# Two transformer blocks in one launch: who makes the last tile sum of a seven-product set, and where the activation sums are made

## The reference, cut to what matters

```python
hf = rms_norm(x, g_ffn[layer])
x = x + (jax.nn.silu(hf @ w_gate[layer]) * (hf @ w_up[layer])) @ w_down[layer]
...
h2 = rms_norm_2(x, g_ffn[i])
x = x + (jax.nn.silu(h2 @ w_gate[i]) * (h2 @ w_up[i])) @ w_down[i]
```

## Time and profile before

| what | value |
|---|---|
| median of 3 runs | 2364.06 us (2363.55 to 2365.42) |
| the profiled execution, its own time | 2367.7 us |
| its span in the trace | 2365.9 us |
| granted TensorE clock, mean | 0.998 of full |
| busy: PE, weight loads, DVE | 99%, 83%, 82% |
| busy: ACT, POOL | 52%, 17% |

### The profile page before, as it was taken

The page is one execution under the profiler, slowest core; times in us unless marked ns, Lnnn a source line. Parts: engine busy times, 40 slices in busy tenths (PEclk is TensorE's granted clock), DMA queues, the critical chain, the costliest instruction groups (busy, mean ns, idle before and its releaser), DMA issues.

```text
span 2365.9 us, 30942 instructions
## 1 busy us (share of the span) xinstructions
PE 2352.9 (99%) x10692; PEld 1957.8 (83%) x10692; DVE 1948.9 (82%) x2542; ACT 1223.9 (52%) x1639; POOL 403.6 (17%) x290
## 2 busy tenths in 40 slices
PE   9999999999999999999999999999999999999999
PEld 8988888878888788888888888888888888888887
DVE  7788887889888877878897976988988897787885
ACT  6554555645454544545654445455545454464553
POOL 1000000130534335200000000013053433520000
PEclk9999999999999999999999999999999999999999
DMA  8755455656766666665655564566575766665655
GB/s 304 238 176 186 153 170 167 222 196 189 248 203 233 204 228 226 213 213 187 195 196 196 178 196 160 194 239 204 186 251 198 242 213 236 216 214 200 212 190 168
DMA packets 130338, 487.44 MB, mean 206 GB/s; under 512 B 14480, under 2 KB 15120, under 8 KB 129568
## 3 DMA queue, kind: packets, MB, share of 16 engines
q1 hardware_dynamic: 116736, 421.32, 53.6%
q0 software_dynamic: 13184, 64.02, 7.6%
q10 hardware_dynamic: 288, 0.33, 0.0%
HBM read 483.51 MB, written 2.10 MB: 205 GB/s over the span
## 4 chain that ended last, share of the span: by engine, by line
PE 65%; DVE 3%; issue 0%; ACT 0%; ACTq 0%; DVEq 0%
PE acc L627 43%; PE po L627 7%; PE pt L627 6%; PE acc L774 3%; PE pt L774 2%; PE po L774 2%; DVE w_lo L1654 1%; DVE tmp_c L1789 1%; PE acc L664 0%; PE po L965 0%; PE acc L904 0%; PE acc L889 0%; PE po L973 0%; DVE tmp_b L1709 0%; ACT w_hi L1145 0%
## 5 line engine op out<-in xcount | busy, mean ns | idle before, releaser
L1654 DVE TENSOR_TENSOR w_lo<-raw,w_hi 128x1024 fp32r<-128x1024 f32 x796 | 1033.3, 1313 | 299.0 <-ACT w_hi L1145 292.2
L1145 ACT ACTIVATE w_hi<-raw 128x1024 fp32r<-128x1024 f32 x795 | 833.4, 1058 | 797.9 <-PE acc L627 499.2
L627 PE MATMUL acc<-w_hi,norm_hi 128*128 128x512 f32 (+1 forms) x1460 | 568.5, 390 | 0.1
L627 PE MATMUL acc<-w_hi,norm_lo 128*128 128x512 f32 (+1 forms) x1460 | 565.3, 387 | 0.0
L627 PE MATMUL acc<-w_lo,norm_hi 128*128 128x512 f32 (+1 forms) x1460 | 387.5, 387 | 0.0
L627 PE MATMUL acc<-w_hi,mix_hi 128*128 128x512 f32 x832 | 325.1, 391 | 0.8 <-DVE mix_lo L2153 0.8
L627 PE MATMUL acc<-w_hi,mix_lo 128*128 128x512 f32 x832 | 324.0, 389 | 0.0
L627 PEld LDWEIGHTS acc<-w_hi,norm_hi 128*128 128x128 f32 x1460 | 274.2, 188 | 55.8 <-issue 0.8
L627 PEld LDWEIGHTS acc<-w_hi,norm_lo 128*128 128x128 f32 x1460 | 274.2, 188 | 55.1
L627 PEld LDWEIGHTS acc<-w_lo,norm_hi 128*128 128x128 f32 x1460 | 272.9, 188 | 56.0 <-DVE w_lo L1654 0.2
L627 PE MATMUL acc<-w_lo,mix_hi 128*128 128x512 f32 x832 | 222.6, 389 | 0.2 <-DVE w_lo L1654 0.2
(11 more groups left out here) (354 smaller groups left out, 2934.8 us busy)
## 6 DMA issues: line engine op xcount, KB each, us to landing
raw<-stream SPq DMA_DIRECT2D x795, 512.0 KB, 3.7
heads<-seven_in POOLq DMA_DIRECT2D x48, 768.0 KB, 6.9
heads<-seven_in POOLq DMA_DIRECT2D x12, 512.0 KB, 7.4
tab<-seven_in POOLq DMA_DIRECT2D x12, 512.0 KB, 7.4
heads<-x_in POOLq DMA_DIRECT2D x4, 512.0 KB, 9.0
x<-x_tok POOLq DMA_DIRECT2D x4, 512.0 KB, 7.1
x<-mem_tok POOLq DMA_DIRECT2D x2, 1024.0 KB, 6.6
x<-x_tok POOLq DMA_DIRECT2D x1, 2048.0 KB, 10.1
```

Of the source, the lines that this page charges most:

```text
L627: last = pe.matmul(out_[:, c * NB:c * NB + width], a[:, k * T + c * P:k * T + (c + 1) * P], w[:, s, kk * width:(kk + 1) * width], start=cl ...
L1145: act.activation(w_hi[:, (units.fixed - 1) % RING, :], src, ACT.Copy).then_inc(w_hi_ready, 1)
L1654: dve.tensor_tensor(w_lo[:, s, :], src, w_hi[:, s, :].bitcast(F32), ALU.subtract)\
```

## The change

There are three edits.

1. POOL makes three of the four sums of a step. The fourth, the last tile, is made by DVE for both steps at once, as one subtraction of 128x1024 (`last_sums`), placed right ahead of part 0 of `seven_lo`. It waits for the load of the last tile and for POOL's sums of both steps. ACT's copy of the last tile (line 1245) waits for it (`last_summed`).
2. The norm sums move from pair (0, "up", 1) to the end of the pair before it. In (0, "up", 1) the parts of `seven_lo` stand at splits 6, 8 and 10 instead of 6, 8 and 11.
3. The hidden sums of group 1 move from pair (1, "up", 2) to (1, "up", 1). In both pairs that have hidden sums `sums_raw` stays at split 9; `sums_lo` goes from 11 to 14, where it is behind `take_up` (13), and ACT's `sums_hi` from 10 to 13.

```diff
+HIDDEN_SUMS = ((0, 2), (1, 1))
...
             def seven_sums(j):
                 for step in range(STEPS):
-                    own = 3 * (STEPS * j + step)
+                    own = 2 * (STEPS * j + step)
                     pool.wait_ge(seven_landed[step], 16 * (j + 1))
                     after_own(pool.tensor_tensor(raw7(step, T3), raw7(step, T2), raw7(step, T1), ALU.subtract), own + 1)
                     after_own(pool.tensor_tensor(raw7(step, T1), raw7(step, T1), raw7(step, W11), ALU.subtract), own + 2)
-                    after_own(pool.tensor_tensor(raw7(step, T2), raw7(step, T2), raw7(step, T1), ALU.subtract), own + 3)
-                    pool.wait_ge(last_landed, 16 * (j + 1))
-                    pool.tensor_tensor(last_raw(j)[:, step], last_raw(j)[:, step], raw7(step, T2), ALU.subtract)\
-                        .then_inc(seven_summed, 1)
+                    pool.tensor_tensor(raw7(step, T2), raw7(step, T2), raw7(step, T1), ALU.subtract).then_inc(seven_summed, 1)
...
+                    act.wait_ge(last_summed, j + 1)
                     act.activation(last_hi(), last_raw(j), ACT.Copy).then_inc(seven_hi_ready, 1)
...
+            def last_sums(j):
+                dve.wait_ge(last_landed, 16 * (j + 1))
+                dve.wait_ge(seven_summed, STEPS * (j + 1))
+                dve.tensor_tensor(last_raw(j), last_raw(j), both_steps(heads, T2), ALU.subtract).then_inc(last_summed, 1)
...
             def seven_lo(j, part):
                 dve.wait_ge(seven_hi_ready, 3 * j + part + 1)
+                if part == 0:
+                    dve.wait_ge(last_summed, j + 1)
...
-                    return {} if j is None else {k: [lambda i=i: seven_lo(j, i)] for i, k in enumerate(at)}
+                    one, two, last = at
+                    return {one: [lambda: last_sums(j), lambda: seven_lo(j, 0)], two: [lambda: seven_lo(j, 1)],
+                            last: [lambda: seven_lo(j, 2)]}
...
                             wait_rows()
                             gated()
-                            split(3)
+                            split(1)
+                            sums_hi(False)
+                            split(2)
...
-                            sums = {10: [lambda: sums_hi(True)]} if p == 2 and g < LAST_GROUP else {}
+                            sums = {2 * NU - 3: [lambda: sums_hi(True)]} if (g, p) in HIDDEN_SUMS else {}
...
                         if (g, p) == (0, 0):
                             during(2 * NU - 3, at)
+                            sums_raw(False, which * N_SEVEN)
                             gated(2 * NU - 2)
                             split(2)
+                            sums_lo(False)
                             take_up(2)
                             split(1)
...
-                            if p == 2 and g < LAST_GROUP:
-                                sums = {9: [lambda: sums_raw(True, used)], 11: [lambda: sums_lo(True)]}
+                            if (g, p) in HIDDEN_SUMS:
+                                sums = {9: [lambda: sums_raw(True, used)], 2 * NU - 2: [lambda: sums_lo(True)]}
```

More of the change, by code:

```diff
@@ L305, in two_blocks @@
         seven_summed = sem("seven_summed")
+        last_summed = sem("last_summed")
         seven_hi_ready = sem("seven_hi_ready")
@@ L1320, in mlp @@
                         if j is None:
-                            sums = {7: [gated], 9: [lambda: sums_hi(False)]}
-                            steps(2 * NU, both(early, preparing(after, 5, 6, 8), sums, joining(after, 13)))
+                            steps(2 * NU, both(early, preparing(after, 5, 6, 8), {7: [gated]}, joining(after, 13)))
                         else:
-                            sums = {10: [lambda: sums_hi(True)]} if p == 2 and g < LAST_GROUP else {}
+                            sums = {2 * NU - 3: [lambda: sums_hi(True)]} if (g, p) in HIDDEN_SUMS else {}
                             if after is None and g < LAST_GROUP:
@@ L1923, in preparing @@
                 def preparing(j, *at):
-                    return {} if j is None else {k: [lambda i=i: seven_lo(j, i)] for i, k in enumerate(at)}
+                    if j is None:
+                        return {}
+                    one, two, last = at
+                    return {one: [lambda: last_sums(j), lambda: seven_lo(j, 0)], two: [lambda: seven_lo(j, 1)],
+                            last: [lambda: seven_lo(j, 2)]}
                 def joining(j, at):
@@ L1977, in mlp @@
                         if j is None:
-                            sums = {7: [lambda: sums_raw(False, which * N_SEVEN), gated],
-                                    10: [lambda: sums_lo(False)], 2 * NU - 1: [take_up]}
-                            steps(2 * NU, both(early, preparing(after, 6, 8, 11), joining(after, 13), sums))
-                        else:
-                            sums, used = {}, which * N_SEVEN + (SEVEN.index((g, "up", 2)) if g < LAST_GROUP else 0)
-                            if p == 2 and g < LAST_GROUP:
-                                sums = {9: [lambda: sums_raw(True, used)], 11: [lambda: sums_lo(True)]}
+                            ends_ = {7: [gated], 2 * NU - 1: [take_up]}
+                            steps(2 * NU, both(early, preparing(after, 6, 8, 10), joining(after, 13), ends_))
+                        else:
+                            sums, used = {}, which * N_SEVEN + SEVEN.index(pair)
+                            if (g, p) in HIDDEN_SUMS:
+                                sums = {9: [lambda: sums_raw(True, used)], 2 * NU - 2: [lambda: sums_lo(True)]}
                             ready_ = joining(after, 11)
```

## The result

The changed kernel is slower: 2378.05 us (median of 4 runs, 2373.91 to 2381.44) against 2363.81 us; ratio 1.0057, 95% interval 1.0045 to 1.0069. The forecast was 2372.0 with a range to 2380.5, slower with a chance of 0.50. The direction held, and so did the wide range, but the time lies 1 us above the forecast's own range (2367 to 2377): the forecast rise was 7.9 us and the measured one is 14.2.

A forecast was written before the change was run, and what follows sets the result against it. PE is busy 99% of the span, so only PE's waits count. Gains 10.2 less costs 7.0 + 3.2 + 7.9 = 18.1 gave net +7.9 us: 2372.0 against the 2364.06 median, own range 2367 to 2377, wide range 2355.5 to 2380.5.

The forecast's parts named there:

- 18.1 of costs: DVE work at the new places makes PE wait: norm sums 7.0, hidden sums 3.2, last tile sum 7.9 us.
- 10.2 of gains: PE waits in four MLP windows go: 5.2 us at late set openings, 5.0 behind (1, "up", 2).
- the 5.0 us of edit 3: Behind (1, "up", 2), `take_up` no longer comes late and the waits go: 4.1 + 0.9 us gained.
- The openings: Sets 0 and 12 open late, PE waiting for `sums_lo`; moving the norm sums gains 4.1 + 1.1 = 5.2 us.
- Cost of edit 1: `last_sums` behind `mix_lo`, 1.26 us each, delays splits behind part 0 in twelve of 24 sets: 7.9 us.
- four have 0.95: In four pairs DVE has 0.95 us of room behind `mix_lo`, so the last tile sum costs 0.3 each, 1.2.
- The walk: Norm sums beside POOL, held four or five times: `take_up` 5.0 us late, PE waits 3.3; edit 2 costs 7.0.
- The clock fall of 1.7: Behind the 3.3 us PE wait after the moved norm sums, first MLP, a slower PE clock costs 1.7 us.
- `sums_lo` behind `take_up` adds 1.22: Moved hidden sums: about 1.3 us late at `take_up` plus 1.22; PE waits 1.9, second MLP 1.3, 3.2 in all.
- POOL's shorter train: Two fewer POOL subtractions relieve DVE by 0.26 us in each of the five tightest pairs behind part 0.
- The rival that both balance: Last tile sum costs 7.9, norm sums 1.0, hidden sums 1.2: 10.1 against 10.2, 2364.0 us; chance 0.28.
- The rival that DVE has the room: Stalls simply go; costs 0.7 for `last_sums`, 0 norm sums, 0.9 + 0.3 hidden sums: 2355.8 us; chance 0.22.

The follow-up runs named there:

- the first train later: The changed kernel with GpSimd's sums of sets 0 and 12 started at unit 17 of the MLP instead of unit 12; 2371.26 us, 1.0032 of before.
- edit 1 alone with the early place: The kernel before with only edit 1, its last tile sum one split earlier, ahead of the split before `mix_lo`; 2362.10 us, 0.9993 of before.

## Why the prediction was right in direction, and short by 6 us

The forecast was 18.1 of costs less 10.2 of gains, +7.9. The traces give 19.9 of new waits less the 8.1 of the kernel before as traced again, +11.8, and the two traced runs lie 11.0 apart. The medians give +14.2. The traced run of the changed kernel is its fastest, 4.1 under the median, and no trace shows what its other runs lose. The direction was no luck: it rests on edit 1, whose cost goes when its sum is left out or moved up. That the costs came out near 18.1 is luck in part, since edit 1 was put 3.7 too low and edit 2 3.5 too high.

**Gains: 10.2 forecast, 5.2 at the places counted.** The step that failed is the 5.0 us of edit 3. I read it from a single trace whose span of 2365.9 is longer than that of every other run of that kernel here (the longest has 2365.6, the usual ones are near 2362). In the second trace the wait behind (1, "up", 2) and both clock falls are missing; of the places counted for edit 3 only 1.1 us in the second MLP are left. The openings are there in both (5.6 us, 4.1 in the second trace) and went in full. The other 2.9 of the 8.1 stand at places that the working did not count, such as 0.7 us at 602 and 0.6 at 816, and the changed kernel's trace has no wait there. The working said that the trace lay 3.6 us over the median and took that off both kernels alike; it should have asked which rows made up the 3.6. They were among those that I had counted as gain.

**Cost of edit 1: 7.9 forecast, 11.6 in the trace** (10.7 alone, 13.7 by leaving the sum out). The mechanism held: no room behind `mix_lo`, twelve pairs, 1.22 us each time. What failed is "four have 0.95". That room does not belong to the pair. In (1, "up", 1) of the kernel before it was there. These are the splits around `take_up`, then the two behind part 0 and the weight load that needs the first of them:

```profile
675.34 1.23 DVE L1654 TENSOR_TENSOR w_lo<-raw,w_hi 128x1024 fp32r<-128x1024 f32 x1 [1.50 <-ACT w_hi L1145]
...
678.42 1.75 DVE L1654 TENSOR_TENSOR w_lo<-raw,w_hi 128x1024 fp32r<-128x1024 f32 x1
680.78 1.62 DVE L1654 TENSOR_TENSOR w_lo<-raw,w_hi 128x1024 fp32r<-128x1024 f32 x1 [0.61 <-ACT w_hi L1145]
...
699.25 2.35 DVE L1654 TENSOR_TENSOR w_lo<-raw,w_hi 128x1024 fp32r<-128x1024 f32 x2
...
701.42 0.19 PEld L627 LDWEIGHTS po<-w_lo,norm_hi 128*128 128x128 f32 x1
```

The split ahead of `take_up` had started 0.4 us before POOL's train, and the two behind it were held by parts of a subtraction only. In the changed kernel the train starts 0.2 us before that split, which takes 2.20:

```profile
673.37 2.20 DVE L1655 TENSOR_TENSOR w_lo<-raw,w_hi 128x1024 fp32r<-128x1024 f32 x1 [1.49 <-ACT w_hi L1144]
```

The two behind `take_up` take 4.49 (the row of 676.93 above). From the start of the split ahead of `take_up` to the end of the second behind it pass 8.05 us instead of 7.07. The room is gone, and the wait is 1.32 instead of 0.3. When POOL's train starts is set by the landing of its load and by PE, so the rooms change from run to run: the pair near 746 waits 1.5 us in the changed kernel and 0.6 with edit 1 alone, and the pair near 700 waits 1.3 and 1.1, and 0.3 with the first train later.

**Cost of edit 2: 7.0 forecast, 3.5 in the trace** (2.4 and 1.1). The walk had the holds right: POOL held all five sums once in the first MLP, and three of them in the second, as forecast. It had a hold too dear. One cost 1.0 us, so the five took 7.9, where the walk had some 9 (from 469.6 to 478.3 or 478.7); `take_up` came 3.9 late and not 5.0, and PE waited 2.3 us instead of 3.3. The clock fall of 1.7 did not come in this run. It does come behind the same wait in the trace of the kernel without the last tile sum:

```profile
495.00:500.00 5.00, 4.51 (x13) 3.55 (x14) 4.84 (x5) 5.00 (x5) 0.00 (x0) 0.66 0.60 193
```

That the late train brought 6.8 us by medians, twice the waits of the trace, I can't settle. Clock falls in the other runs may be a part: the four runs of the changed kernel have mean granted clocks of 1.000, 0.998, 0.997 and 0.999, the first is the traced one, and the trace of before with its two falls has 0.998.

**Cost of edit 3: 3.2 forecast, 3.9 in the trace** (2.2 and 1.7 early in (1, "up", 2)). The step "`sums_lo` behind `take_up` adds 1.22" left out that POOL holds that one too (2.31), though the same text had it for the splits beside it. The last 0.9 of the 19.9, at the opening at 1729, belongs to none of the edits by these traces. PE waits there for `combine`; edit 2 alone has 0.7 at the same place, edit 1 alone with the early place 1.0, and the kernel before, traced again, has its 0.7 at 602, the same opening of the first MLP.

**The rest.** POOL's shorter train gave VectorE busy time back (24 sums of 1.22 are 29.3 us, and it rose by 18.1), but PE's waits behind part 0 show nothing of it: they came in twelve pairs, as forecast, and larger. It mattered for edit 2: the expectation for edit 2 alone had put the train of eight at only "a little more". The wait of part 0 for POOL's sixth sum cost nothing. The rival that both balance fell with the gain. The rival that DVE has the room fell as it was put, and was right one split further up.

## What to carry to other kernels

On an engine that runs a list in order, the place of a new instruction is worth more than its length: find the last idle time ahead of the first consumer that has no room, and put it before that idle time ends, not behind it. Before a stall in one trace is counted as a gain, ask whether the median run has it; here the trace that lay above the median had waits that the next one lacked. A chain of short instructions on VectorE did worst beside GpSimd here, since each link let one of GpSimd's instructions in.

## What the runs showed of the hardware that was not expected

- The same wait at the same place can be followed by a clock fall or not: the late opening of set 0 (2.8 us between weight loads in both traces of the kernel before) has the granted clock at 0.68 over the next 5 us in one and at 1.00 in the other. The window of 500 to 550 lacks 18 matmuls with the fall and 11 without, so it cost 7 of them, 1.6 us. In all fourteen traces, 23 waits of 1.9 us or more stand in the MLPs, and the clock fell to 1.2 GHz behind ten of them.
- The one that started first held the other. In the kernel before, at (1, "up", 2), the two splits took 4.23 us and POOL's first subtraction 1.29 in one trace, 2.35 and 2.16 in the other.
- GpSimd got one 128x512 subtraction in at each link of the chain: sums of 0.42 us lasted 1.40, the 1.23 us one 2.20, while GpSimd's own 1.29 us became only 1.35 to 1.46 beside the short ones. GpSimd lost almost nothing there, VectorE 5 us in all.
- Transposes of VectorE were not held. In the trace of before the 158 that ran beside a subtraction of GpSimd took 0.42 to 0.44 us each, and so did the 722 others.
